# A causal depthwise convolution on the matmul engine: four token phases of 32 channels in place of two of 64, and its layer norm by tokens

## The chip, the cores and the metric

The kernel runs on one core of a Trainium2 chip. Its time is the device time of one execution in microseconds. The number to predict is the median of several runs. The engines are TensorE (PE, with its weight loads as PEld), VectorE (DVE), ScalarE (ACT), GpSimd (POOL) and SyncE (SP, which here only issues transfers).

## The reference

Two transformer-like blocks follow each other, each with two layers, on 256 tokens of width 1024, all in float32. The change touches only the mixer of the first block, twice (layers 0 and 1). One mixer projects the normed tokens, and from the projection it makes three parts: sparse attention (512 wide), a gated depthwise convolution (256 channels) and a pooled part (256 wide). The three go through `w_out`.

```python
def conformer_conv(u, conv_dw, conv_b, ln_g, ln_b, conv_pw):
    a, g = jnp.split(u, 2, axis=-1)
    y = a * jax.nn.sigmoid(g)
    y = lax.conv_general_dilated(          # 31 taps, causal, one filter for each of 256 channels
        y, conv_dw[:, None, :], window_strides=(1,), padding=[(CONV_KERNEL - 1, 0)],
        dimension_numbers=('NWC', 'WIO', 'NWC'), feature_group_count=CONV_WIDTH)
    y = y + conv_b
    y = jax.nn.silu(layernorm(y, ln_g, ln_b))          # over the 256 channels of a token
    return jnp.einsum('bsc,cd->bsd', y, conv_pw)

        mix = jnp.concatenate([y_attn, y_conv, y_pool], axis=-1)
        mix = jnp.einsum('bse,ed->bsd', mix, w_out[i])
        h = h + rmsnorm(mix, norm_mix_post[i])
```

## The kernel before

The program is written engine by engine: each engine has its own instruction list, and the lists wait for each other through counted semaphores (`nxt(name)` waits for the next count of a semaphore, `do(..., counts[name])` raises it, `settle()` waits for the engine's own latest result). No scheduler moves anything, so the order in the code is the order on the engine.

**Weights.** All large weights stream through SBUF in chunks of 1 MB (128 partitions of 2048 values), each loaded in two halves. ScalarE copies a half to a rounded high part (`prep`, tile `whi`, 128x1024), VectorE subtracts it from the original to get a low part (`lo`, tile `wlo`), and TensorE multiplies high by high, high by low and low by high, three matmuls in the place of one float32 matmul (`wide_tile`). `lo(s)` on VectorE's list therefore stands between its other work, and TensorE waits for it (`arrive`). A chunk of index `s0 + 11` is the first one of `w_out` (`s0` counts from the layer's first input chunk), `s0 + 14` its last.

**The stage of the mixer.** TensorE's list in this stage is: scores of head pairs 0 to 3 (`scores`), tap matmuls of the convolution laid between them (`taps`, as many as `TAPS_AT` says at each of five places), the turned probabilities (`turn_probs`), the products with the values (`mix_values`), and then the chunks of `w_out` (`tail`). A score goes to VectorE (`masked`: mask and row maximum), to ScalarE (`exps`) and back to VectorE (`scaled`: divide by the sum) before `turn_probs` can take it; `scores(p)` may only start when `masked(p - 1)` has read the banks.

**The convolution before.** The gated input is turned to channels by tokens, with even tokens in 64 partitions and odd tokens in the other 64 (`YT`, `YC`; 4 groups of 64 channels). One tap matmul holds a 128x128 block of taps as weights and streams 128 token pairs; 16 shifts for each of 4 groups make 64 matmuls in plain float32 a layer. The result lies channels by tokens in `acc[:, 3]`. The layer norm over channels then runs across partitions: a matmul with a matrix of 1/256 (`means`, L2058) gives the mean, VectorE subtracts it (L1264), ScalarE squares, a second matmul (L2073) gives the variance, GpSimd takes the power -0.5 (L487), VectorE spreads it (L1276), a third matmul (L2081) turns it, VectorE multiplies (L1280), ScalarE applies gain, bias and silu (L737), and 16 matmuls (`conv_out`, L2094) apply `conv_pw`. VectorE splits their result (`split`, L1172 and L1174) for the last chunk of `w_out`. Before its first half (128 tokens) of `w_out`, TensorE calls `ready(i)` for each of 8 blocks of 128 features in the order attention 0, 1, pool 0, 1, attention 2, 3, convolution 0, 1.

**Tap weights.** Each layer has 8 pieces of 8 taps (512 KB), loaded by SyncE into a ring of 4 (`load_taps`); while SyncE waits to issue a piece, the weight chunks behind it in its list wait too.

**Layer 0 alone** has one more step: after the split of the convolution VectorE computes rotary angles (`angles_by_feature`), and ScalarE's sines of these stand ahead of the squares of the norm that follows `w_out`.

## Time and profile before

| | us |
|---|---|
| median of 3 runs | 2320.17 (2319.89 to 2320.49) |
| time of the profiled execution | 2319.79 |
| its span (first to last instruction) | 2318.0 |
| TensorE busy in it | 2296.8 (99%) |
| VectorE busy in it | 1540.9 (66%) |
| ScalarE busy in it | 1221.5 (53%) |
| mean share of the DMA engines in use by the weights' queue | 56.4% |

The span is one profiled execution; what lies around it is the 1.8 us between 2318.0 and 2319.79. A time that is saved or lost on TensorE's list shows one to one in the span, since TensorE is hardly ever idle.

### The profile page before, as it was taken

What the parts mean: (1) busy time and instruction counts of PE and PEld (TensorE: products, weight loads), DVE (VectorE), ACT (ScalarE), POOL (GpSimd) and SP (SyncE); (2) the same over time, 40 slices, a digit from 0 to 9 for tenths busy, and PEclk for the clock granted to TensorE, in tenths of its full rate; (3) what the DMA queues carried; (4) which work ended last, traced back from release to release, by engine and by line L of the source; (5) the groups of instructions that cost most, each with busy time, mean ns of one, the idle gap of its engine ahead of it and who ended that gap; (6) DMA issues with size and microseconds to landing.
All of it is one profiled execution on the core that took longest, in us unless ns stands there. A gap on an engine that the chain in (4) does not pass through costs nothing.

```text
span 2318.0 us, 30390 instructions
## 1 busy us (share of the span) xinstructions
PE 2296.8 (99%) x12124; PEld 1959.9 (85%) x12124; DVE 1540.9 (66%) x2019; ACT 1221.5 (53%) x1788; POOL 79.1 (3%) x134
## 2 busy tenths in 40 slices
PE   8999999999999999999999999999999999999998
PEld 6888888888888888988888888888889888888887
DVE  6867657776566667876575665665678765756664
ACT  6645446464455556755444554554567553445553
POOL 0110000100000000000000000000000000000000
PEclk9999999999999999999999999999999999999999
DMA  8437655456656555645665465565556456554652
GB/s 334 146 119 238 198 171 209 146 170 203 211 163 217 189 172 163 206 162 183 218 199 191 157 217 192 179 221 190 173 164 214 153 183 221 195 193 164 199 193 89
DMA packets 119805, 434.91 MB, mean 188 GB/s; under 512 B 13553, under 2 KB 13809, under 8 KB 119665
## 3 DMA queue, kind: packets, MB, share of 16 engines
q1 hardware_dynamic: 119664, 432.96, 56.4%
q8 instruction: 97, 1.59, 0.3%
q14 instruction: 44, 0.35, 0.0%
HBM read 431.86 MB, written 1.05 MB: 187 GB/s over the span
## 4 chain that ended last, share of the span: by engine, by line
PE 95%; DVE 4%; ACT 1%; issue 0%; POOL 0%; DMA 0%; DVEq 0%; POOLq 0%; ACTq 0%
PE ub L1716 21%; PE ub L1713 11%; PE ub L1684 9%; PE ub L1686 9%; PE ub L1685 9%; PE acc L1684 8%; PE acc L1685 8%; PE acc L1686 8%; PE ub L1691 1%; PE ub L1692 1%; PE ub L1693 1%; PE acc L1747 1%; DVE wlo L1020 1%; DVE work L1208 1%; PE acc L2162 0%; DVE best L1205 0%
## 5 line engine op out<-in xcount | busy, mean ns | idle before, releaser
L1020 DVE TENSOR_TENSOR wlo<-raw,whi 128x1024 fp32r<-128x1024 f32 x776 | 913.1, 1220 | 215.2 <-ACT whi L534 213.4
L534 ACT ACTIVATE whi<-raw 128x1024 fp32r<-128x1024 f32 x776 | 777.3, 1052 | 200.9 <-PE ub L1686 140.5
L1716 PE MATMUL ub<-xhl,whi 128*128 128x512 f32 x2176 | 514.6, 390 | 0.0
L1716 PEld LDWEIGHTS ub<-xhl,whi 128*128 128x128 f32 x2176 | 404.2, 188 | 82.7 <-issue 1.3
L1684 PE MATMUL acc<-whi,bhl 128*128 128x512 f32 x736 | 288.2, 392 | 0.0
L1685 PE MATMUL acc<-wlo,bhl 128*128 128x512 f32 x736 | 286.6, 389 | 0.0
L1686 PE MATMUL acc<-whi,bhl 128*128 128x512 f32 x736 | 286.5, 389 | 0.0
L1684 PE MATMUL ub<-whi,xhl 128*128 128x512 f32 (+1 forms) x704 | 275.3, 391 | 3.0 <-DVE wlo L1020 1.5
L1713 PEld LDWEIGHTS ub<-xhl,wlo 128*128 128x128 f32 x2176 | 272.0, 191 | 6.2
L1713 PE MATMUL ub<-xhl,wlo 128*128 128x256 f32 x2176 | 275.4, 283 | 0.0
L1686 PE MATMUL ub<-whi,xhl 128*128 128x512 f32 (+1 forms) x704 | 272.5, 387 | 0.0
L1685 PE MATMUL ub<-wlo,xhl 128*128 128x512 f32 (+1 forms) x704 | 272.4, 387 | 0.0
L1686 PEld LDWEIGHTS acc<-whi,bhl 128*128 128x128 f32 x736 | 138.2, 188 | 29.0
L1684 PEld LDWEIGHTS acc<-whi,bhl 128*128 128x128 f32 x736 | 138.3, 188 | 27.9
L1685 PEld LDWEIGHTS acc<-wlo,bhl 128*128 128x128 f32 x736 | 138.3, 188 | 27.4
L1684 PEld LDWEIGHTS ub<-whi,xhl 128*128 128x128 f32 x704 | 132.7, 189 | 30.7 <-issue 1.8
L1686 PEld LDWEIGHTS ub<-whi,xhl 128*128 128x128 f32 x704 | 132.6, 188 | 26.6
L1685 PEld LDWEIGHTS ub<-wlo,xhl 128*128 128x128 f32 x704 | 132.8, 189 | 25.2
L1427 DVE TENSOR_TENSOR tX<-tS,ub 128x512 f32<-128x512 f32 x72 | 49.5, 687 | 132.6 <-ACT tS L839 132.4
L839 ACT ACTIVATE tS<-ub 128x512 f32<-128x512 f32 x72 | 43.0, 597 | 149.2 <-PE ub L1713 124.6
L1684 PE MATMUL ub<-whi,bhl 128*128 128x512 f32 x256 | 99.8, 390 | 0.0
L1686 PE MATMUL ub<-whi,bhl 128*128 128x512 f32 x256 | 99.6, 389 | 0.0
(305 smaller groups left out, 2471.7 us busy)
## 6 DMA issues: line engine op xcount, KB each, us to landing
raw<-in_w SPq DMA_DIRECT2D x776, 512.0 KB, 5.0
gain<-in_gains SPq DMA_DIRECT2D x20, 512.0 KB, 7.8
tapw<-in_taps SPq DMA_DIRECT2D x16, 512.0 KB, 4.3
DEC<-in_decay SPq DMA_DIRECT2D x2, 768.0 KB, 8.1
par<-in_par SPq DMA_DIRECT2D x2, 647.0 KB, 9.4
par<-in_par SPq DMA_DIRECT2D x2, 556.0 KB, 7.2
H<-in_x SPq DMA_DIRECT2D x2, 512.0 KB, 4.5
out_h<-H SPq DMA_DIRECT2D x4, 256.0 KB, 2.6
```

The costliest lines, as they stand in the source:

```text
L534: do(act.activation(whi[:, s % RING, c], raw[:, slot, c], ACT.Copy), counts["w_hi"])
L839: do(act.activation(units(tS[:, j % 2, :]), ub[:, 2 * (j % 2):2 * (j % 2) + 2, 0:S], ACT.Copy), counts["a_out"])
L1020: do(dve.tensor_tensor(wlo[:, s % RING, c], raw[:, PLACES[s][0], c], whi[:, s % RING, c].bitcast(f32), ALU.subtract), counts["w_lo"])
L1208: do(dve.match_replace(after[:, c0:c1], best[:, t, :], cur[:, c0:c1], TAKEN))
L1427: do(dve.tensor_tensor(units(tX[:, j % 2, :]), units(tS[:, j % 2, :]), ub[:, 2 * (j % 2):2 * (j % 2) + 2, S:2 * S], ALU.add), counts["us"])
L1684: pe.matmul(o, x_h, w_h, start=first, stop=False, skip_group_check=True)
L1685: pe.matmul(o, x_h, w_l, start=False, stop=False, skip_group_check=True)
L1686: return pe.matmul(o, x_l, w_h, start=False, stop=last, skip_group_check=True)
L1691: pe.matmul(o, w_h, x[:, 0, :], start=first, stop=False, skip_group_check=True)
L1692: pe.matmul(o, w_h, x[:, 1, :], start=False, stop=False, skip_group_check=True)
L1713: last = pe.matmul(bank[:, S:], wlo[:, s % RING, n:n + P], xhl[:, kt, 0, :], start=first, stop=stop, skip_group_check=True)
L1716: last = pe.matmul(bank, whi[:, s % RING, n:n + P], xhl[:, kt, :, :].rearrange("p a n -> p (a n)"), start=first, stop=stop, skip_group_che ...
```

## The change

Tokens now lie in four phases (token number modulo 4) of 32 partitions each, so 128 partitions hold 32 channels, and 8 groups of channels with 9 shifts make 72 tap matmuls a layer. The operands change places: the shifted input (64 quads of tokens, 64 columns) is the weight, and the 128x128 block of taps streams. The result lies by tokens: 64 partitions (quads), and in the free dimension 4 phases of 256 channels, gathered from two banks. The layer norm then runs along the free dimension: VectorE adds the bias as it reads the banks (`biased`), sums (L1262) and negates the mean (L1264), ScalarE squares with an accumulated sum (4 instructions), GpSimd takes the power, VectorE applies mean and deviation (4 instructions, L1280), TensorE turns the result to channels by tokens (`turn_normed`, 8 transposes), ScalarE applies gain, bias and silu, and `conv_out` is 4 matmuls of 256 columns. Both are called inside the first half of `w_out`: `turn_normed` ahead of block 4, `conv_out` ahead of block 5 (before: `last_values` after block 1, `conv_out` ahead of block 4). `TAPS_AT` puts 40 of the taps between the first and the second scores. VectorE's `lo` of the chunks `s0 + 12` to `s0 + 14` moves later in its list, and ScalarE's `prep(s0 + 14)` too. There are 9 tap pieces, and the ring has 5.

```diff
-GROUPS = 4
-SHIFTS = 16
+GROUPS = 8
+SHIFTS = 9
...
-TAP_RING = 4
-PAIRS = S // 2
+TAP_RING = 5
+QUADS = S // 4
 RSPAN = 384
-TAPS_AT = (16, 16, 12, 12, 8)
+TAPS_AT = (40, 16, 8, 8, 0)
...
                             sp.wait_ge(sem["dots_done"], IDX_HEADS * (L + 1))
-                            load_taps(L, 2, PIECES)
+                            load_taps(L, 2, 4)
+                            sp.wait_ge(sem["ze"], 7 * L + 7)
+                            load_taps(L, 4, PIECES)
...
-                    def even_and_odd(b):
+                    def phases():
 
                         nxt("yt_done")
-                        for i in range(2):
-                            r = slice(64 * i, 64 * i + 64)
-                            src = acc[r, b, :].rearrange("p (g m i) -> p g m i", g=2, i=2)[:, :, :, i]
-                            do(act.activation(YC[r, 2 * b:2 * b + 2, SHIFTS - 1:], src, ACT.Copy),
-                               counts["yc_ready"] if i else None)
+                        for g in range(4):
+                            src = acc[32 * g:32 * g + 32, 0, :].rearrange("p (f m i) -> p f m i", f=2, i=4)
+                            for i in range(4):
+                                do(act.activation(YC[32 * i:32 * i + 32, 2 * g:2 * g + 2, SHIFTS - 1:], src[:, :, :, i], ACT.Copy),
+                                   counts["yc_ready"] if i == 3 else None)
...
-                        if p == 1:
-                            prep(s0 + 14)
...
-                    nxt("ha_ready")
-                    do(act.activation(tS[:, 0, :], wide(cacc, 0, GROUPS), ACT.Square), counts["sq_ready"])
+                    nxt("cneg_ready")
+                    for j in range(4):
+                        do(act.activation(tS[0:QUADS, j // 2, (j % 2) * S:(j % 2 + 1) * S], cacc[0:QUADS, j, :], ACT.Square,
+                                          bias=cneg[0:QUADS, j:j + 1], accum_out=csq[0:QUADS, j:j + 1]),
+                           counts["sq_ready"] if j == 3 else None)
+                    attended(1)
                     act.wait_ge(sem["spare_ready"], 1)
                     do(act.activation(spare[:, 1:2], spare[:, 0:1], ACT.Silu))
...
+                    prep(s0 + 14)
+                    nxt("ct_done")
+                    for f in range(2):
+                        do(act.activation(cact[:, f, :], ub[:, 2, f * S:(f + 1) * S], ACT.Silu,
...
...
+                    def biased():
+
+                        dve.wait_ge(sem["par_in"], 16 * (L + 1))
+                        dve.wait_ge(sem["pool_out"], L + 1)
+                        dve.wait_ge(sem["tap_used"], PIECES * (L + 1))
+                        for b, bank in enumerate((3, 1)):
+                            row = par1[0:QUADS, P1["conv_b"] + b * P:P1["conv_b"] + (b + 1) * P]
+                            do(dve.tensor_tensor(
+                                cacc[0:QUADS, :, cols(b)].rearrange("p j (g c) -> p g j c", c=32),
+                                acc[0:QUADS, bank, :].rearrange("p (g j c) -> p g j c", g=4, c=32),
+                                row.rearrange("p (g c) -> p g c", c=32).unsqueeze(2).broadcast_to([QUADS, 4, 4, 32]),
+                                ALU.add), counts["c_ready"])
+
                     masked(0)
                     masked(1)
                     scaled(0)
-                    lo(s0 + 12)
+                    lo(s0 + 12, 0)
                     masked(2)
                     scaled(1)
-                    lo(s0 + 13, 0)
                     masked(3)
                     scaled(2)
-                    lo(s0 + 13)
+                    lo(s0 + 12)
+                    biased()
                     scaled(3)
-                    lo(s0 + 14, 0)
...
+                    do(dve.tensor_reduce(csum[0:QUADS, :], cacc[0:QUADS, :, :], AX.X, ALU.add))
+                    settle()
+                    do(dve.tensor_scalar(cneg[0:QUADS, :], csum[0:QUADS, :], -1.0 / S, None, ALU.mult), counts["cneg_ready"])
                     attended_lo(0)
+                    lo(s0 + 13, 0)
                     nxt("aux_ready")
...
+                    attended_lo(1)
+                    lo(s0 + 13)
+                    nxt("rstd_ready")
+                    settle()
+                    for j in range(4):
+                        do(dve.tensor_scalar(cacc[0:QUADS, j, :], cacc[0:QUADS, j, :], cneg[0:QUADS, j:j + 1],
+                                             crs[0:QUADS, j:j + 1], ALU.add, ALU.mult),
+                           counts["cn_ready"] if j == 3 else None)
                     lo(s0 + 14)
-                    nxt("rstd_ready")
...
...
-                            last = pe.matmul(acc[:, 3, cols(g)], tapw[piece % TAP_RING][:, k, :], YC[:, g, q:q + PAIRS],
-                                             start=q == 0, stop=q == SHIFTS - 1)
+                            last = pe.matmul(acc[0:QUADS, (3, 1)[g % 2], cols(g // 2)], YC[:, g, q:q + QUADS],
+                                             tapw[piece % TAP_RING][:, k, :], start=q == 0, stop=q == SHIFTS - 1)
...
+                    def turn_normed():
+
+                        nxt("cn_ready")
+                        fill(U_[2], "sig_ready")
+                        for f in range(2):
+                            for j in range(4):
+                                c = f * S + j * QUADS
+                                last = pe.transpose(ub[:, 2, c:c + QUADS], cacc[0:QUADS, j, cols(f)],
+                                                    ident[0:QUADS, 0:QUADS])
+                        give(last, "ct_done")
...
                     def made(i):
                         if i == 4:
+                            turn_normed()
+                        if i == 5:
                             conv_out()
                         pe.wait_ge(sem["prod_ready"], 4 * L + i // 2 + 1)
                     tail(so, lambda i: OUT_ORDER[i], acc_bank, lambda: turn(0, acc_bank, XN1, "xn_ready"),
-                         ready=made, first=last_values, early=1)
+                         ready=made)
```

Smaller edits: the turned input has 4 transposes in place of 8, the gated product on VectorE is written once instead of twice (256 columns instead of 512), GpSimd no longer fills `means`, and the parameter block is smaller (`P1` ends at 1030 in place of 1294).

The first place is TensorE's list in layer 0, from the first scores to the first turned probabilities (`L1900` and `L1901` are the scores, `L2003` the turned probabilities, `L2036` the taps). Before:

```order
L1901 MATMUL ub<-KK,Q 128x256
L2036 MATMUL acc<-YC,tapw_95 128x128 x8
L2036 MATMUL acc<-YC,tapw_96 128x128 x8
L1900 MATMUL ub<-KK,Q 128x128
L1901 MATMUL ub<-KK,Q 128x256
L1900 MATMUL ub<-KK,Q 128x128
L1901 MATMUL ub<-KK,Q 128x256
L2036 MATMUL acc<-YC,tapw_97 128x128 x8
L2036 MATMUL acc<-YC,tapw_98 128x128 x8
L2003 MATMUL ub<-cst,sm 128x128 x6
```

Now (the scores are L1901 and L1902, the turned probabilities L2002):

```order
L2036 MATMUL acc<-tapw_92,YC 64x128 x8
L2036 MATMUL acc<-tapw_93,YC 64x128 x8
L2036 MATMUL acc<-tapw_94,YC 64x128 x8
L2036 MATMUL acc<-tapw_95,YC 64x128 x8
L2036 MATMUL acc<-tapw_96,YC 64x128 x8
L1901 MATMUL ub<-KK,Q 128x128
L1902 MATMUL ub<-KK,Q 128x256
L1901 MATMUL ub<-KK,Q 128x128
L1902 MATMUL ub<-KK,Q 128x256
L2036 MATMUL acc<-tapw_92,YC 64x128 x8
L2036 MATMUL acc<-tapw_93,YC 64x128 x8
L2002 MATMUL ub<-cst,sm 128x128 x6
```

The second scores stand behind 40 taps instead of 16; of the 72 taps only 16 are left for the places behind the second turned probabilities and the third scores.

The second place is VectorE's list in layer 0 behind the third `scaled` (`L1237` and `L1240` are `scaled`, `L1020` is `lo`, `L1264` the mean's subtraction, `L1246` the low part of an attention block, `L1269`, `L1172` and `L1174` the pooled part). Before:

```order
L1020 TENSOR_TENSOR wlo<-raw,whi 128x1024
L1237 RECIPROCAL rinv<-rsum 128x4
L1240 TENSOR_TENSOR sm<-sm,rinv 128x2x128
L1240 TENSOR_TENSOR sm<-sm,rinv 128x2x256
L1020 TENSOR_TENSOR wlo<-raw,whi 128x1024
L1264 TENSOR_TENSOR cacc<-cacc,acc 128x512
L1246 TENSOR_TENSOR bhl<-acc,bhl 128x512
L1269 TENSOR_SCALAR tX<-ub,par_75 128x256 x2
L1172 CAST bhl<-tX 128x512
L1174 TENSOR_TENSOR bhl<-tX,bhl 128x512
```

Now (`L1225` and `L1228` are `scaled`, `L1010` is `lo`, `L1244` is `biased`):

```order
L1010 TENSOR_TENSOR wlo<-raw,whi 128x1024
L1244 TENSOR_TENSOR cacc<-acc,par_74 64x4x4x32 x2
L1225 RECIPROCAL rinv<-rsum 128x4
L1228 TENSOR_TENSOR sm<-sm,rinv 128x2x128
L1228 TENSOR_TENSOR sm<-sm,rinv 128x2x256
L1262 TENSOR_REDUCE cstat<-cacc 64x4
L1264 TENSOR_SCALAR cstat<-cstat 64x4
L1234 TENSOR_TENSOR bhl<-acc,bhl 128x512
L1010 TENSOR_TENSOR wlo<-raw,whi 128x1024
L1269 TENSOR_SCALAR tX<-ub,par_74 128x256 x2
L1160 CAST bhl<-tX 128x512
L1162 TENSOR_TENSOR bhl<-tX,bhl 128x512
```

The bias additions now stand ahead of the last `scaled`, and the sum over channels between it and the attention block.

The third place is TensorE's list in the first half of `w_out`, around the end of the convolution. Before, with `conv_out` as L2094:

```order
L1684 MATMUL acc<-whi,bhl 128x512
L1685 MATMUL acc<-wlo,bhl 128x512
L1686 MATMUL acc<-whi,bhl 128x512
L2094 MATMUL ub<-cact,par_75 128x128 x16
L1684 MATMUL acc<-whi,bhl 128x512
```

Now, with the 8 transposes as L2071 and `conv_out` as L2082:

```order
L2071 MATMUL ub<-cst,cacc 128x64 x8
L1685 MATMUL acc<-whi,bhl 128x512
L1686 MATMUL acc<-wlo,bhl 128x512
L1687 MATMUL acc<-whi,bhl 128x512
L1685 MATMUL acc<-whi,bhl 128x512
L1686 MATMUL acc<-wlo,bhl 128x512
L1687 MATMUL acc<-whi,bhl 128x512
L2082 MATMUL ub<-cact,par_74 128x256 x4
L1685 MATMUL acc<-whi,bhl 128x512
```

Between the 8 transposes and `conv_out` stands one block of `w_out` (6 matmuls); ahead of the last two blocks only one block is left behind `conv_out`, where there were two.

## Rows read from the trace of the kernel before

**Rows 1.** The page, part 1: busy us (share of the span) xinstructions, whole execution.

```profile
PE 2296.8 (99%) x12124; PEld 1959.9 (85%) x12124; DVE 1540.9 (66%) x2019; ACT 1221.5 (53%) x1788; POOL 79.1 (3%) x134
```

**Rows 2.** Two stretches (layers 0, 1): length, busy us by engine, clock, DMA share, GB/s.

```profile
85.33:128.70 43.37, 41.58 (x320) 34.78 (x320) 33.36 (x66) 20.77 (x54) 9.47 (x10) 1.00 0.50 171
421.50:464.90 43.40, 41.67 (x321) 34.80 (x320) 30.43 (x57) 20.92 (x55) 9.47 (x10) 1.00 0.49 170
```

**Rows 3.** Timeline of TensorE, layer 0: start, us, line, shapes, xcount, [idle before <-releaser].

```profile
86.19 3.84 PE L2036 MATMUL acc<-YC,tapw 128*128 128x128 f32 x32
...
101.13 0.87 PE L2003 MATMUL ub<-cst,sm 128*128 128x128 f32 x6 [0.94 <-DVE sm L1240]
101.94 0.50 PE L1900 MATMUL ub<-KK,Q 64*128 64x128 f32 x4
...
102.80 0.87 PE L2017 MATMUL acc<-turned_w,V 128*64 128x256 f32 x8
103.60 2.94 PE L2036 MATMUL acc<-YC,tapw 128*128 128x128 f32 x24
106.38 0.82 PE L2003 MATMUL ub<-cst,sm 128*128 128x128 f32 x6
```

**Rows 4.** Timeline of TensorE in two very narrow windows, inside the first value products.

```profile
103.07 0.39 PE L2017 MATMUL acc<-turned_w,V 128*64 128x256 f32 x2
...
103.28 0.39 PE L2017 MATMUL acc<-turned_w,V 128*64 128x128 f32 x4
```

**Rows 5.** Timeline of TensorE, layer 0: the norm's matmuls and `conv_out`.

```profile
111.43 1.06 PE L2058 MATMUL acc<-cacc,means 128*128 128x128 f32 x8
...
114.08 1.05 PE L2073 MATMUL acc<-means,tS 128*128 128x2 f32 x8
...
117.92 0.49 PE L2081 MATMUL acc<-cst,spread 128*128 128x128 f32 x2
...
121.09 2.06 PE L2094 MATMUL ub<-cact,par 64*128 64x128 f32 x32
```

**Rows 6.** Timeline of VectorE, layer 0: mask, scale, `lo`, attention block, pooled part.

```profile
102.93 0.96 DVE L1225 SCALAR_TENSOR_TENSOR sm<-ub,bias 128x768 f32<-128x768 f32 x1 [0.71 <-PE ub L1901]
...
105.05 1.03 DVE L1240 TENSOR_TENSOR sm<-sm,rinv 128x256 f32<-128x256 f32 x2
105.99 1.22 DVE L1020 TENSOR_TENSOR wlo<-raw,whi 128x1024 fp32r<-128x1024 f32 x1
...
113.18 0.68 DVE L1246 TENSOR_TENSOR bhl<-acc,bhl 128x512 fp32r<-128x512 f32 x1
113.78 0.87 DVE L1269 TENSOR_SCALAR tX<-ub,par 128x256 f32<-128x256 f32 x2
...
115.75 0.15 DVE L1273 TENSOR_SCALAR cvar<-acc 128x2 f32<-128x2 f32 x1
```

**Rows 7.** Groups by line and form, 80 to 140 us: xcount | busy us, mean ns.

```profile
L699 ACT ACTIVATE sm<-sm,rmax 128x256 f32<-128x256 f32 x8 | 3.9, 494 | 0.0
L1230 DVE TENSOR_REDUCE rmax<-sm 128x2 f32<-128x512 f32 x4 | 2.7, 676 | 0.0
L487 POOL TENSOR_TENSOR crs<-cvar,half 128x2 f32<-128x2 f32 x1 | 1.6, 1621 | 21.3 <-DVE cvar L1273 21.3
L1108 DVE TENSOR_SCALAR ang<-posf,cst 128x256 f32<-128x256 f32 x1 | 0.4, 353 | 0.0
```

**Rows 8.** The page, part 6: tap transfers, xcount, KB each, us to landing.

```profile
tapw<-in_taps SPq DMA_DIRECT2D x16, 512.0 KB, 4.3
```

**Rows 9.** Timeline of VectorE, layer 0: the convolution's split, the next norm's product.

```profile
123.92 0.69 DVE L1174 TENSOR_TENSOR bhl<-ub,bhl 128x512 fp32r<-128x512 f32 x1
...
135.22 1.41 DVE L1061 SCALAR_TENSOR_TENSOR XN<-H,rh,gain 128x512 f32<-128x512 f32 x2 [2.05 <-POOL rh L443]
```

**Rows 10.** Timeline of TensorE, layer 0: last `w_out` chunk, then the transposes of XN.

```profile
125.94 0.39 PE L1684 MATMUL acc<-whi,bhl 128*128 128x512 f32 x1
...
136.82 0.38 PE L1747 MATMUL acc<-cst,XN 128*128 128x128 f32 x2
```

154 lines of the change are left out of this document (50 added, 104 removed).

## The prediction

> **What bounds the kernel now.** I read the page's busy shares first: TensorE is busy for 2296.8 us, 99% of the span, VectorE for 66% [rows 1]. So a change counts by what it adds to TensorE's own work, and by how much longer it makes TensorE wait. Then I read the busy time of the stage that the change touches, from the first scores to the end of the first half of `w_out` [rows 2]. It lasts 43.37 us in layer 0 and 43.40 in layer 1, TensorE is busy in 41.58 and 41.67 of it, so idle for 1.79 and 1.73; the clock is granted in full (1.00). The layers behave alike; I work out layer 0 and double it. Last I read TensorE's and VectorE's timelines in the stage: TensorE's idle time stands ahead of scores and turned probabilities, as the 0.94 ahead of 101.13 that VectorE's `scaled` ended [rows 3], and VectorE waits for TensorE's scores in turn, 0.71 ahead of 102.93 [rows 6]. The tap matmuls are what TensorE does meanwhile.
>
> **TensorE's own work, per layer.** Records here: a float32 matmul leaves two, a transpose one.
>
> Taps. 32 records take 3.84, 24 take 2.94 [rows 3]: 0.90/8, so 0.1125 each, and 64 taps cost 128 x 0.1125 = 14.4. With 64 columns as weights and 128 streamed columns the value products are the nearest rows: 256 streamed columns at 103.07 are followed by 128-column ones at 103.28, 0.21 later [rows 4]; four records of 128 columns end within 0.39, two side by side, and with a record's own length of about 0.27 (0.38 for the 256-column one, less 0.11) the pairs stand 0.11 to 0.12 apart. The time follows the streamed columns, and they stay 128. I take 0.11: 72 x 2 x 0.11 = 15.8, which is 1.4 more. Bounds: the present spacing gives 16.2 (+1.8); the rival below has half.
>
> The other rule about this operation speaks for the change. The Trainium skill, "TensorE: Matmul & The Clock Gate", section "LDWEIGHTS (loading the stationary operand)", says that a weight load's time goes with its columns, about columns/1.2 ns. By it the 64-column load is 53 ns against 107 (an estimate from that page), and if the load set the pace the taps would take 7.7 us a layer instead of 15.8. The trace bears half of it out, as the next sentences show.
>
> Variance matmuls stream only 2 columns and still stand (1.05 - 0.25)/7 = 0.114 apart [rows 5], the pace of the taps. So for 128 columns of weights the load alone costs as much as the stream, and halving it leaves the stream as the bound.
>
> Gone: 4 of 8 transposes, at (0.82 - 0.27)/5 = 0.11 each [rows 3], 0.44; the mean's 8 records 0.9 (1.06 less the tail), the variance's 0.92, the turn of the deviation 0.3 [rows 5]. Added: 8 transposes, no dearer than 0.11 each, with two changes of matmul type about 1.1 (bounds 0.6 and 1.3). `conv_out` goes from 32 records in 2.06 less the tail [rows 5] to 8 with 256 columns at 0.215, 1.8: 0.2 less. Sum: 1.4 + 1.1 - 0.44 - 0.9 - 0.92 - 0.3 - 0.2 = **-0.3**. TensorE's own work stays where it was.
>
> **TensorE's waits, per layer.** `TAPS_AT` puts 40 taps ahead of the second scores: 8.8 us, which covers `masked(0)` fully, so the present wait there goes. But VectorE has nothing to do meanwhile, and what it does later is then in a row with TensorE. Prices from VectorE's rows: from the start of `masked` at 102.93 to the end of `scaled` at 105.05 + 1.03 is 3.15 [rows 6], 3.25 with the hand-overs. On TensorE scores take 102.80 - 101.94 = 0.86, value products 0.80, turned probabilities 0.75 [rows 3], 8 taps 1.76; a change between kinds of matmul costs 0.1 (the pairs at 103.28 and 103.39 would be followed at 103.50, the taps start at 103.60 [rows 3, 4]), two of them around a run of taps 0.2.
>
> - Second turned probabilities: VectorE needs 3.25 behind the third scores, TensorE has 8 taps, 1.95. Wait **1.3**.
> - Third: behind the fourth scores again 3.25, TensorE has value products and 8 taps, 2.75. Wait **0.5**.
> - Fourth: behind `scaled(2)` VectorE has half a `lo`, 1.14 (1.22 less the overlap [rows 6]), `biased`, not in the trace, nearest the 128x512 subtraction from a bank, 0.60 from 113.18 to 113.78 [rows 6], twice 1.2 (bounds 1.1 and 2.0), and `scaled(3)` 1.15: 3.5. TensorE has 0.75 + 0.80 + 0.80, and 0.1 for a copy: 2.45. Wait **1.0** (and the 0.1).
> - The transposes of the normed result: behind `scaled(3)` VectorE works without a gap: sum over 4 x 256, from the 512-element maximum of 0.676 [rows 7] at one more ns an element 1.2 (bounds 1.0 and 1.6), mean 0.2, low part 0.6, half a `lo` 1.14, pooled part 115.75 - 113.78 = 1.97 [rows 6], variance 0.1, low part 0.6, half a `lo` 1.14, then 4 `tensor_scalar` of 256: nearest 0.353 [rows 7], overlapped 0.28, 1.1 (bounds 0.8 and 1.9). Together 8.05. TensorE has 0.75, pooled product 1.0, 0.80 and 24 matmuls of `w_out` at 10.88/48 = 0.227 (125.94 to 136.82 holds 48 [rows 10]) with 0.1: 8.1. A tie, but GpSimd's power lies beside the last low parts: 1.62 for 2 columns [rows 7], now 4, so 1.6 to 3.2; I take 1.9. Wait **0.2**.
> - Last block: VectorE's split of `conv_out`, 1.4, against one block of `w_out`, 1.4. Wait **0.1**.
>
> Sum 3.2, before 1.8: **+1.4**. With the work, **+1.1 to +1.2** a layer, 2.3 for both.
>
> **Layer 0 alone.** The split ended at 124.61, and TensorE needed it at 125.94 [rows 9, 10]: 1.3 of slack. From the split's end, angles, sines, squares and GpSimd's root led to XN at 136.63, 12.0 later [rows 9]; TensorE asked for it 10.9 after 125.94 [rows 10]. Now TensorE takes up the last block as the split ends, so the lead of 1.3 is gone: the first half of XN is ready 11.35 after, the second 12.0, against 10.9 and 11.8. Wait 0.5 + 0.2 = **0.7** (bounds 0 and 1.3). Layer 1 has no angles there, and nothing waits.
>
> **What costs nothing.** ScalarE's 16 small copies in place of 4: bounded above by the 0.494 of a 256-column one [rows 7], 4 take 2.0, and TensorE has half of the pool projection (24 matmuls, 0.11 each at least) and 0.86 of scores before the first tap; the other groups are needed 4 us apart. Without that cover the first tap would be up to 2.0 late. VectorE's two `lo` of the last chunk, 2.3, now come behind the four scalings, and TensorE has the 8 transposes, `conv_out` and two blocks, 5.8, before it needs them; without that cover they would be on the path. ScalarE's `prep` for them is done before. The tap pieces: SyncE is held until 32 taps are done, as now, but those now come in one run, so the weights behind them come no later; a piece lands in 4.3 [rows 8], and behind the issue of the last one stand 32 more taps, 7.0, before its own. Less on VectorE in the gated product (0.5) is covered, since the second scores wait for the taps.
>
> **Sum.** The profiled execution took 2319.8 (its span of 2318.0 and 1.8 around it). 2319.8 + 2.3 + 0.7 = 2322.8; the median of the runs, 2320.2, lies 0.4 above that execution. I say **2323.2**.
>
> **Rivals.**
> - *Load-bound taps (faster).* The load of 128 columns takes as long as the taps' spacing [rows 5]; if it is what sets the pace, 64 columns stand 0.055 apart. The 40 taps ahead of the second scores then take 4.4 less, the next 16 gain 0.4 until `scaled(0)` holds them, and at the later places longer waits eat the rest. 1.15 - 4.8 is 3.6 less than before a layer: 2319.8 - 7.2 + 0.7, with the 0.4, 2313.7. The sign turns below about 0.09 a record, 0.2% is passed below about 0.065. The 0.21 for 256 columns [rows 4] speaks against it. 0.06. [...]
> - *VectorE's norm chain is dearer (slower, clearly).* Sum, four scalings and power at their upper bounds add 0.4 + 0.8 + 1.0, `biased` 0.5: each lies on the chain without a gap, so up to 2.5 a layer, 2327 to 2328. For it: three of these prices stand in no row. Against: all of their nearest rows are cheap. 0.22.
> - *The waits don't add up (no change).* VectorE's steps overlap more, or the old waits were as long for the same reasons: 2319.5 to 2321. 0.17.
> - *My sum:* 2321 to 2325. 0.55.
>
> The range 2319.5 to 2327.5 leaves out the fast rival and the end of the slow one; the forecast's own is 2321 to 2325. A measurement of this kernel can tell about 0.2%, 4.6 us, from no change. Slower by more (above 2324.8): most of the slow rival and a tail of mine, 0.26. Faster by more (below 2315.5): 0.05. Within: 0.69.
>
> **What would show it.** Right: tap records about 0.11 apart with 64-column weights; TensorE's idle time in the stage near 3.2, with the longest waits ahead of the second and fourth turned probabilities, all ended by VectorE's `scaled`; VectorE idle for some us ahead of the second `masked`; in layer 0 alone a wait of 0.5 or more at the transposes of XN. Wrong: a spacing near 0.06; a wait above 1 ahead of the 8 new transposes, or one at `conv_out` ended by ScalarE; a first tap that waits for ScalarE's copies.

## The result, and the profile after

The changed kernel takes 2324.16 us (median of 20 runs, 2323.46 to 2325.78); the kernel before, run beside it, 2320.29 (20 runs, 2319.46 to 2321.29). The ratio is 1.0017, with a 95% interval of 1.0011 to 1.0023: 3.9 us slower. The interval lies above 1, so the loss is clear, though it is smaller than the 0.2% that the forecast calls a change that can be told. The profiled execution took 2324.03, its span is 2321.8. The page, part 1, of the changed kernel, in the columns of [rows 1]:

```profile
PE 2295.9 (99%) x12080; PEld 1957.7 (84%) x12080; DVE 1545.4 (67%) x2029; ACT 1226.3 (53%) x1814; POOL 77.9 (3%) x131
```

TensorE works 0.9 us less than in [rows 1] and the span is 3.8 longer: the loss is waiting. Where it lies is read from the stage in layer 0, from the first scores to the start of the last block of `w_out`. First the kernel before, then the changed one (length, PE busy, PEld, DVE, ACT, POOL, clock, DMA share, GB/s):

```profile
85.33:125.94 40.61, 38.82 (x308) 32.49 (x308) 31.12 (x61) 20.45 (x53) 9.47 (x10) 1.00 0.53 182
```

```profile
84.79:127.31 42.52, 38.38 (x290) 31.62 (x289) 32.44 (x62) 21.78 (x61) 8.84 (x10) 1.00 0.51 174
```

TensorE idles 42.52 - 38.38 = 4.14 us where it idled 40.61 - 38.82 = 1.79, and works 0.44 less. Its timeline in the changed kernel names the places (start, us, line, shapes, xcount, [idle before <-releaser]; L1901 are scores, L2002 turned probabilities, L2036 taps, L2071 the transposes of the normed result, L2082 `conv_out`, L1685 blocks of weight chunks, L1748 the transposes of XN). The lines answer to [rows 3, 5, 10]:

```profile
85.65 8.95 PE L2036 MATMUL acc<-tapw,YC 128*64 128x128 f32 x80
94.53 0.50 PE L1901 MATMUL ub<-KK,Q 64*128 64x128 f32 x4
...
99.03 0.87 PE L2002 MATMUL ub<-cst,sm 128*128 128x128 f32 x6
...
104.03 0.88 PE L2002 MATMUL ub<-cst,sm 128*128 128x128 f32 x6 [1.37 <-DVE sm L1228]
...
109.03 0.87 PE L2002 MATMUL ub<-cst,sm 128*128 128x128 f32 x6 [0.72 <-DVE sm L1228]
...
112.50 0.87 PE L2002 MATMUL ub<-cst,sm 128*128 128x128 f32 x6 [0.83 <-DVE sm L1228]
...
120.97 0.68 PE L2071 MATMUL ub<-cst,cacc 64*128 64x64 f32 x8
121.58 0.50 PE L1685 MATMUL acc<-whi,bhl 128*128 128x512 f32 x1
...
123.07 1.89 PE L2082 MATMUL ub<-cact,par 128*128 128x256 f32 x8
124.61 0.58 PE L1685 MATMUL acc<-whi,bhl 128*128 128x512 f32 x1
...
127.31 0.47 PE L1685 MATMUL acc<-whi,bhl 128*128 128x512 f32 x1 [0.95 <-DVE bhl L1162]
...
138.84 1.32 PE L1748 MATMUL acc<-cst,XN 128*128 128x128 f32 x8 [0.39 <-DVE XN L1051]
...
149.12 0.47 PE L1685 MATMUL ub<-whi,xhl 128*128 128x512 f32 x1 [0.76 <-DVE wlo L1010]
```

The 80 tap records stand (8.95 - 0.27)/79 = 0.110 us apart (0.27 is the last one's own length). Two waits of the kernel before, not among its rows above, are needed beside them:

```profile
90.61 0.50 PE L1900 MATMUL ub<-KK,Q 64*128 64x128 f32 x4 [0.58 <-DVE sm L1225]
...
146.30 0.47 PE L1684 MATMUL ub<-whi,xhl 128*128 128x512 f32 x1 [0.26 <-DVE wlo L1020]
```

The wait of 0.58 ahead of the second scores is gone; those ahead of the second to fourth turned probabilities have come for it, and one of 0.95 ahead of the last block. VectorE in the same stretch of the changed kernel:

```profile
95.52 0.96 DVE L1213 SCALAR_TENSOR_TENSOR sm<-ub,bias 128x768 f32<-128x768 f32 x1 [4.51 <-PE ub L1902]
...
110.03 1.27 DVE L1244 TENSOR_TENSOR cacc<-acc,par 64x512 f32<-64x512 f32 x2
...
112.48 1.21 DVE L1262 TENSOR_REDUCE cstat<-cacc 64x4 f32<-64x1024 f32 x1
...
119.49 1.37 DVE L1280 TENSOR_SCALAR cacc<-cacc,cstat 64x256 f32<-64x256 f32 x4
...
125.00 1.07 DVE L1160 CAST bhl<-ub 128x512 fp32r<-128x512 f32 x1 [1.86 <-PE ub L2082]
126.10 1.05 DVE L1162 TENSOR_TENSOR bhl<-ub,bhl 128x512 fp32r<-128x512 f32 x1
```

VectorE idles 4.51 ahead of the second `masked`, while TensorE does its 40 taps; that TensorE waits later for what VectorE could not do then is the theory which the first experiments test. The two instructions of the split, the second of them 0.69 in [rows 9], take 1.07 and 1.05. GpSimd's power for 4 columns (at 117.74) took 1.02, less than the 1.62 for 2 columns in [rows 7].

The sum, by how far TensorE's list lags behind that of the kernel before: the first scores come 0.54 earlier, the last block 1.37 later, the transposes of XN 2.02 later [rows 10], and the block at 149.12 (146.30 before) 2.82 later. In layer 1 the same stage adds 1.96 (the last block at 466.54 against 462.12, the first scores at 424.02 against 421.56), and XN's transposes stand at 477.51 against 473.00. From there the 4.5 stay to the last matmul. From its start to the end of the span it is 6.1 us where it was 6.7, which leaves the 3.8 (3.9 before rounding). These 0.6 us less come back in the trace of every run with the new convolution, against every one with the old; what shortens the end of the program was not looked into. So TensorE's list does not show one to one in the span here: 0.6 of its loss is given back behind it.

### The profile page after: what moved, and what is told of

It reads as the page before. It is cut to its first block, busy times and chain, and to the rows that moved or that the text cites. A ratio compares the mean times of both kernels' runs of the same rounds, so it can differ in the third digit from the quotient of the medians.

```text
span 2321.8 us, 30325 instructions
## 1 busy us (share of the span) xinstructions
PE 2295.9 (99%) x12080; PEld 1957.7 (84%) x12080; DVE 1545.4 (67%) x2029; ACT 1226.3 (53%) x1814; POOL 77.9 (3%) x131
## 3 DMA queue, kind: packets, MB, share of 16 engines
HBM read 432.64 MB, written 1.05 MB: 187 GB/s over the span
## 4 chain that ended last, share of the span: by engine, by line
PE 96%; DVE 2%; ACT 0%; issue 0%; DMA 0%; POOL 0%; SPq 0%; DVEq 0%; POOLq 0%; ACTq 0%
PE ub L1717 21%; PE ub L1714 11%; PE ub L1685 9%; PE ub L1687 9%; PE ub L1686 9%; PE acc L1685 9%; PE acc L1687 8%; PE acc L1686 8%; PE ub L1692 1%; PE ub L1693 1%; PE ub L1694 1%; PE acc L2036 1%; PE acc L1748 1%; DVE wlo L1010 1%; PE ub L1902 0%; PE acc L2152 0%
## 5 line engine op out<-in xcount | busy, mean ns | idle before, releaser
L1010 DVE TENSOR_TENSOR wlo<-raw,whi 128x1024 fp32r<-128x1024 f32 x776 | 913.7, 1221 | 215.0 <-ACT whi L529 213.5
L1685 PE MATMUL acc<-whi,bhl 128*128 128x512 f32 x736 | 288.7, 392 | 1.9 <-DVE bhl L1162 1.9
L1685 PE MATMUL ub<-whi,xhl 128*128 128x512 f32 (+1 forms) x704 | 275.3, 391 | 3.7 <-DVE wlo L1010 1.9
L1685 PEld LDWEIGHTS acc<-whi,bhl 128*128 128x128 f32 x736 | 138.3, 188 | 30.7 <-issue 3.1
L1685 PEld LDWEIGHTS ub<-whi,xhl 128*128 128x128 f32 x704 | 132.7, 188 | 31.6 <-issue 2.3
L1685 PE MATMUL ub<-whi,bhl 128*128 128x512 f32 x256 | 99.8, 390 | 0.0
```

The costliest lines, as they stand in the source:

```text
L1010: do(dve.tensor_tensor(wlo[:, s % RING, c], raw[:, PLACES[s][0], c], whi[:, s % RING, c].bitcast(f32), ALU.subtract), counts["w_lo"])
L1685: pe.matmul(o, x_h, w_h, start=first, stop=False, skip_group_check=True)
```

## The experiments

My theory, from the two traces: three separate things make the new waits. The order of the taps (`TAPS_AT`) gives TensorE 40 taps where fewer would cover VectorE's step, and 8 where VectorE needs about 16; the split writes with a step (its elements do not lie side by side); and in layer 0 the rotary angles, which VectorE computes behind the split, hold what follows. The rivals: the waits are VectorE's work as a whole, which would show elsewhere if one were removed; or the convolution and its norm themselves are dearer. Each time stands beside the kernel before as run on the same chip in the same rounds, whose median was 2320.2 in the first four runs, 2321.4 in the next four, and 2320.3 and 2320.1 in the last. The 95% intervals of these ratios reach about 2 us to either side, so smaller differences between two runs are not shown by the times alone; for them I go by the traces.

**The taps, in both kernels.** The changed kernel with another order:

```diff
-TAPS_AT = (40, 16, 8, 8, 0)
+TAPS_AT = (24, 16, 16, 16, 0)
```

> The changed kernel with TAPS_AT = (24, 16, 16, 16, 0) in place of (40, 16, 8, 8, 0). Mine (the order of the taps, not the convolution itself, costs the waits ahead of the turned probabilities): 24 taps, 5.3 us, still cover the first masked step, VectorE's idle time of 4.51 ahead of the second one falls to about 1.0, and 16 taps, 3.65 with the hand-over, cover the 3.25 that VectorE needs behind the third and fourth scores: the waits of 1.37 and 0.72 go to 0 and 0.1. The fourth, 0.83, goes to 0 to 0.4. 2.3 to 2.9 us a layer, 2318.3 to 2319.6 in all, under the kernel before. Rival (the waits are VectorE's whole work per layer, which no order of the taps shortens, so they come back at the transposes of the normed result): the stage stays as long, waits of 1 to 2 us ahead of the 8 transposes or of conv_out, 2322 to 2324.

2320.13 us, ratio 1.0000 (0.9991 to 1.0008): all of the loss is gone. The three waits of 1.37, 0.72 and 0.83 went, but one of 0.96 came ahead of the first turned probabilities:

```profile
96.79 0.88 PE L2002 MATMUL ub<-cst,sm 128*128 128x128 f32 x6 [0.96 <-DVE sm L1228]
```

Its cause is seen on VectorE (first fence; L1213 and L1218 are `masked`) and GpSimd (second):

```profile
92.25 0.96 DVE L1213 SCALAR_TENSOR_TENSOR sm<-ub,bias 128x768 f32<-128x768 f32 x1 [1.01 <-PE ub L1902]
93.24 1.01 DVE L1218 TENSOR_REDUCE rmax<-sm 128x2 f32<-128x256 f32 x2
...
94.37 2.36 DVE L1228 TENSOR_TENSOR sm<-sm,rinv 128x256 f32<-128x256 f32 x2
96.66 1.21 DVE L1010 TENSOR_TENSOR wlo<-raw,whi 128x1024 fp32r<-128x1024 f32 x1
```

```profile
91.65 3.12 POOL L477 TENSOR_TENSOR PO<-W,cst 64x256 f32<-64x256 f32 x4
94.85 1.33 POOL L480 TENSOR_TENSOR PO<-PO,UP 128x512 f32<-128x512 f32 x1
```

`scaled(0)` now falls beside GpSimd's pooling and takes 2.36, where the later `scaled` take 1.03. So the gain was 3.9 and not 4.6 to 5.8.

The kernel before with the changed kernel's order:

```diff
-TAPS_AT = (16, 16, 12, 12, 8)
+TAPS_AT = (36, 12, 8, 8, 0)
```

> The kernel before with only TAPS_AT = (36, 12, 8, 8, 0) in place of (16, 16, 12, 12, 8), the changed kernel's order for its 64 taps. Mine: the wait of 0.58 ahead of the second scores goes, but 8 taps, 1.8 us, stand where 12 stood ahead of the third and fourth turned probabilities, and VectorE has half a low part more there than in the changed kernel: waits of 1.8 to 2.5 ahead of the third and 1 to 1.5 ahead of the fourth, 1.3 to 2.0 a layer in all, 2323 to 2324.5. Rival (the place of the taps is indifferent, since VectorE's work as a whole decides): 2320 to 2321, with the idle time of TensorE in the stage at 1.8 as before.

2322.94, ratio 1.0013 (1.0004 to 1.0022): 2.8 us slower, with the old convolution. TensorE's waits:

```profile
98.95 0.88 PE L2003 MATMUL ub<-cst,sm 128*128 128x128 f32 x6 [0.39 <-DVE sm L1240]
...
104.51 0.87 PE L2003 MATMUL ub<-cst,sm 128*128 128x128 f32 x6 [1.83 <-DVE sm L1240]
...
109.51 0.88 PE L2003 MATMUL ub<-cst,sm 128*128 128x128 f32 x6 [0.48 <-DVE sm L1240]
```

The pattern follows the order of the taps, whichever convolution they belong to. The two larger waits stand one place earlier than I had written, ahead of the second and third turned probabilities, and the second of them is smaller than my 1 to 1.5.

**The split.** In the changed kernel:

```diff
-split(*(z[:, 4:6, :].rearrange("p f (m j) -> p f j m", j=4) for z in (bhi, blo)),
-      ub[:, 0, :].rearrange("p (f j m) -> p f j m", f=2, j=4), "prod_ready")
+split(*(z[:, 4:6, :].rearrange("p f (m j) -> p f m j", j=4) for z in (bhi, blo)),
+      ub[:, 0, :].rearrange("p (f j m) -> p f m j", f=2, j=4), "prod_ready")
```

> The changed kernel, with only the two instructions that split conv_out taken in the order of the result (channel block, token, phase) in place of (channel block, phase, token), so that they write without a step, as the kernel before did. Mine (the step of four elements on the written side makes each 1.07 and 1.05 us where the kernel before has 0.69): both fall to about 0.69, the split ends 0.7 to 0.75 us earlier, and TensorE's wait ahead of the last block of w_out falls from 0.95 to 0.2 in both layers; XN of layer 0 comes 0.7 earlier too, so its wait stays. 1.4 to 1.6 us faster than the changed kernel, about 2322.6. Rival (the price is that of reading one bank in place of two, or of the pattern of three dimensions, whatever the order): the two stay at 1.05 and the time at 2324. Rival (the wait belongs to what VectorE does ahead, two low parts of a weight chunk): the wait stays near 0.9 although the two get shorter.

2322.62, ratio 1.0011 (1.0002 to 1.0020), 2.5 above the kernel before where the changed one is 3.9 above. What got shorter is in the trace, VectorE's first and then TensorE's:

```profile
125.48 0.69 DVE L1160 CAST bhl<-ub 128x512 fp32r<-128x512 f32 x1 [1.86 <-PE ub L2082]
126.20 0.69 DVE L1162 TENSOR_TENSOR bhl<-ub,bhl 128x512 fp32r<-128x512 f32 x1
```

```profile
127.04 0.47 PE L1685 MATMUL acc<-whi,bhl 128*128 128x512 f32 x1 [0.21 <-DVE bhl L1162]
```

As expected to a tenth: both fell to 0.69, and the wait of 0.95 to 0.21. The other way round in the kernel before, which has two phases and so a step of two elements:

```diff
-split(*(z[:, 4:6, :].rearrange("p f (m j) -> p f m j", j=2) for z in (bhi, blo)),
-      ub[:, 0:2, 0:S].rearrange("p j (f m) -> p f m j", f=2), "prod_ready")
+split(*(z[:, 4:6, :].rearrange("p f (m j) -> p f j m", j=2) for z in (bhi, blo)),
+      ub[:, 0:2, 0:S].rearrange("p j (f m) -> p f j m", f=2), "prod_ready")
```

> The kernel before with its split of conv_out taken by channel block, phase and token, so that it writes with a step of two elements (8 bytes) and reads each bank in a row, the other way round than it does. The changed kernel writes with a step of four (16 bytes) and takes 1.07 and 1.05 in place of 0.69. Theory A (each element that is written into another group of 16 bytes pays): with two elements in a group they stay at 0.69. Theory B (any step on the written side pays): above 0.8. In either case TensorE has 1.3 of slack ahead of the last block, and the time stays at 2320 to 2321.

A single run, 2319.97, and both instructions stay at 0.69:

```profile
123.41 0.69 DVE L1172 CAST bhl<-ub 128x512 fp32r<-128x512 f32 x1 [3.46 <-PE ub L2094]
124.14 0.69 DVE L1174 TENSOR_TENSOR bhl<-ub,bhl 128x512 fp32r<-128x512 f32 x1
```

So for this split a step of 8 bytes on the written side is free, and one of 16 costs half as much again (1.07 and 1.05 against 0.69): theory A. The order of reading is not the cause: the changed kernel and this run both read their banks in a row, one at 1.07 and the other at 0.69. The Trainium skill, "SBUF — State Buffer", section "Door 1: The DMA port swizzle (why `[64,N]` ≈ `[32,N]`)", says that SBUF has lines of 16 bytes, that two accesses in a row to a line are needed for full speed, and that each crossing to a new line pays. These three measurements agree; where the same place counts steps of up to 4 float32 as free, they do not, since the step of 4 is the one that paid.

**The angles of layer 0.** First into VectorE's idle time (the cut leaves out the lines that give their tiles other places, three in `tX`):

```diff
...
                     masked(0)
+                    if L == 0:
+                        angles_by_feature()
                     masked(1)
...
-                    if L == 0:
-                        angles_by_feature()
                     for t in range(2):
```

> The changed kernel with the angles of layer 0 (3.8 us of VectorE) computed ahead of the second masked step, where VectorE idles 4.51, in place of behind the split of conv_out; three of their tiles lie in tX for that, two in the place of the old result of the convolution. Mine (the angles and the sines behind them are what makes layer 0 dearer than layer 1): no new wait at the second masked step, ScalarE squares as soon as the first 12 matmuls of the last block are done, 1.7 earlier, the waits of 0.4 and 0.25 ahead of the two halves of XN's transposes go, and of the 0.76 ahead of w_lo at 149 at least 0.5. 1.0 to 1.4 us faster than the changed kernel, 2322.8 to 2323.2. Rival (the chain of squares, root and XN behind the last block decides by itself): 0 to 0.3.

2324.76, ratio 1.0021 (1.0012 to 1.0029): 4.6 above the kernel before, where the changed one is 3.9 above. These 0.7 lie inside the interval, and the trace does not show them: from the first scores of layer 0 to the transposes of XN in layer 1 TensorE's list takes 392.6 us, and 392.7 in the changed kernel. So nothing was gained. On VectorE two instructions of the same form and size:

```profile
92.63 0.76 DVE L1069 TENSOR_SCALAR tX<-tX 128x256 f32<-128x256 f32 x1
...
97.80 0.29 DVE L1080 TENSOR_SCALAR ycos<-tX 128x256 f32<-128x256 f32 x1
```

The first stands beside GpSimd's pooling, the second behind its end at 96.2. The angles took 6.9 in place of 3.8 and put a wait of 2.0 ahead of the first turned probabilities:

```profile
101.41 0.88 PE L2002 MATMUL ub<-cst,sm 128*128 128x128 f32 x6 [2.00 <-DVE sm L1228]
```

The waits at XN and at `w_lo` did go, so this run does not tell what the angles are worth. The next one puts them where GpSimd stands still: among the last `w_down` chunks of the feed-forward stage (number 12, and ScalarE's sines at 13). The cut shows VectorE's part; the tiles lie in the place of `trig2`:

```diff
...
                             lo(min(s + 3, sf + 31))
+                            if L == 0 and j == 12:
+                                angles_by_feature()
```

> The changed kernel with only the angles of layer 0 and their sines moved to the last w_down chunks of the first feed-forward stage. Where the angles stood in the run before, beside GpSimd's pooling, they took 6.85 us in place of 3.75, which hid the gain behind a new wait of 2.0; here GpSimd stands still. Mine (in layer 0 the angles hold the squares of the last block, XN and the low parts behind them): the waits of 0.39 and 0.25 ahead of the transposes of XN and of 0.76 ahead of w_lo go, 1.3 to 2.1 us faster than the changed kernel, 2322.0 to 2322.9; the angles take 3.75 again. Rival (the chain of squares and root holds XN alone): 0 to 0.3.

2323.34, ratio 1.0009 (1.0001 to 1.0018), 1.9 above the kernel before. TensorE's waits from 120 to 160 us (total, times, longest):

```profile
PE acc L1685 <- DVE bhl L1162: 1.0, 1, 1.0
PE ub L2071 <- issue: 0.2, 1, 0.2
```

The changed kernel has 0.4 at XN and 0.8 at `w_lo` there too. So the angles were worth 2.0 us, in layer 0 alone; the table further down has 2.07 from the traces. (The median itself, 2323.34, lies above the 2322.0 to 2322.9 that I expected: in these rounds the kernel before took 1.2 longer too.)

**The taps themselves.** Two of the four output phases are left out here:

```diff
-last = pe.matmul(acc[0:QUADS, (3, 1)[g % 2], cols(g // 2)], YC[:, g, q:q + QUADS],
-                 tapw[piece % TAP_RING][:, k, :], start=q == 0, stop=q == SHIFTS - 1)
+c = (g // 2) * P
+last = pe.matmul(acc[0:QUADS, (3, 1)[g % 2], c:c + 64], YC[:, g, q:q + QUADS],
+                 tapw[piece % TAP_RING][:, k, 0:64], start=q == 0, stop=q == SHIFTS - 1)
```

> The changed kernel with 64 of the 128 columns streamed in each tap matmul, so that two of the four output phases of the convolution are left out; the 64 columns of weights stay. Mine (the streamed columns set the pace, the load of the weights ran beside them at half their time): a record goes from 0.110 to 0.055 to 0.06, 40 taps end 4.3 to 4.4 earlier, VectorE's steps then set the stage, with 1 us more of wait ahead of the first turned probabilities: about 3.4 a layer, 2317 to 2318. Rival (a record costs 0.11 whatever its columns, as the 2-column variance matmuls with 128 columns of weights did): the spacing stays 0.11, the time 2324.

A single run, 2321.94. The spacing was as I said, the time was not. TensorE's timeline:

```profile
85.86 4.88 PE L2037 MATMUL acc<-tapw,YC 128*64 128x64 f32 x80
...
100.95 1.54 PE L2002 MATMUL ub<-cst,sm 128*128 128x128 f32 x6 [2.69 <-DVE sm L1228]
102.43 0.81 PE L1901 MATMUL ub<-KK,Q 64*128 64x128 f32 x4
```

(4.88 - 0.22)/79 = 0.059 a record with both sides at 64 columns, 0.110 with 64 of weights and 128 streamed, 0.1125 with 128 on both [rows 3]. So with 64 columns of weights it is not their load that sets the pace of the taps but the streamed columns. The first turned probabilities came 3.6 earlier (95.45 against 99.03), as expected; then the second waited 2.69, and what stood behind that wait ran slower (the last section comes back to it), so that 1.7 were left at the last block.

**The edits together,** the first step towards a better version:

> The changed kernel with three edits together: the split of conv_out in the order of its result (minus 1.5 by itself), TAPS_AT = (24, 16, 16, 16, 0) (minus 4.0 by itself), and the angles of layer 0 moved from behind the split to the last w_down chunks of the first feed-forward stage, in the place of trig2, where they are needed only at the end of the layers. If the three waits are separate: 2324.2 - 1.5 - 4.0 - 1.4 to 2.1 = 2316.6 to 2317.3, faster than the kernel before by 0.12 to 0.16%. Rival (each is only handed on to the next wait): no better than the best single edit, 2320. TensorE's idle time from the scores to the last block of w_out 1.1 to 1.5 a layer, all of it the wait ahead of the first turned probabilities (0.96) and the last block (0.2).

2317.99, ratio 0.9987 (0.9978 to 0.9996), 3.4 under the kernel before, which was 1.2 slower in these rounds than in those I had worked from. Against the changed kernel, 3.9 above the kernel before, the three edits gain 3.9 - 2.5 = 1.4 (split), 3.9 (taps) and 3.9 - 1.9 = 2.0 (angles), 7.3 in all, and together 3.9 + 3.4 = 7.3. With intervals of 2 us to either side, that the times agree to a tenth is luck. The traces say the same without them, by when TensorE starts the first scores of layer 0 and the transposes of XN in layer 1:

| | scores, layer 0 | XN, layer 1 | between | gain |
|---|---|---|---|---|
| changed kernel | 84.79 | 477.51 | 392.72 | |
| split by token | 85.28 | 476.49 | 391.21 | 1.51 |
| taps later | 85.01 | 473.68 | 388.67 | 4.05 |
| angles late | 84.80 | 475.45 | 390.65 | 2.07 |
| all three | 84.56 | 469.71 | 385.15 | 7.57 |

The single gains add up to 7.63, and together they give 7.57: they are separate waits, not one that moves.

**The old convolution with a better order,** first the taps, then the angles as well (the same edit as above):

```diff
-TAPS_AT = (16, 16, 12, 12, 8)
+TAPS_AT = (20, 16, 16, 12, 0)
```

> The kernel before with only TAPS_AT = (20, 16, 16, 12, 0) in place of (16, 16, 12, 12, 8): the last 8 taps move ahead, to the places where TensorE waits. Mine: 4 more taps, 0.9, cover the 0.58 ahead of the second scores, 4 more cover the 0.94 ahead of the second turned probabilities, and the place without taps stays covered by value products: 1.2 to 1.5 a layer, 2317.2 to 2318, so a better order of the taps gives the old convolution as much as the new one, and the convolution itself is worth nothing. Rival (the later start of the second scores is handed on, as VectorE's steps beside GpSimd are slow): 0.5 a layer or less, 2319 to 2320.

> The old convolution with the same surroundings, for a comparison of the two at their best: TAPS_AT = (20, 16, 16, 12, 0), which by itself was 3.0 under the kernel before, and the angles moved to the last w_down chunks. Only a wait of 0.25 ahead of w_lo was left in that run in layer 0, so 0 to 0.4 is to be gained: 3.0 to 3.4 under the kernel before. If so, and the run with GpSimd's pooling later comes out at 5.0 to 5.4 under it, the new convolution is worth 1.6 to 2.4 us once the waits around it are gone, and the forecast's term for TensorE's own work (minus 0.3 a layer) was too small; if both come out alike, the term was right or too large.

The taps alone: 2318.45, 3.0 under the kernel before (ratio 0.9987, 0.9978 to 0.9996), as much as the 1.2 to 1.5 a layer that I expected. With the angles: 2316.56, 3.8 under it (0.9985, 0.9976 to 0.9994) where I had expected 3.0 to 3.4, and the list of TensorE's waits from 84 to 152 us is empty.

**GpSimd's pooling.** To the run with three edits one wait is added on GpSimd, ahead of its four multiplications:

```diff
                     settle()
+                    pool.wait_ge(sem["scaled"], 4 * L + 1)
                     for f in range(2):
```

> The three edits of the run with split, taps and angles together, and one more: GpSimd's four multiplications of the pooled sums wait until VectorE has scaled the first two heads' probabilities. In that run scaled(0), two instructions with both operands in SBUF, took 2.36 us beside GpSimd in place of 1.03, and TensorE waited 0.96 ahead of the first turned probabilities. If GpSimd is the cause: scaled(0) takes 1.03, the wait of 0.96 falls below 0.1 in both layers, the half of w_lo behind it takes longer (up to 2.3 in place of 1.22), which the 0.7 us of idle time ahead of masked(2) and the 16 taps mostly cover: 1.5 to 1.9 us faster than that run, 5.0 to 5.4 under the kernel before. Rival (the delay is only moved to w_lo, masked(2) and the second turned probabilities): a wait of 0.5 to 1.0 there, 0 to 0.5 faster. Rival (scaled(0) is slow for another reason, such as the first use of the tile): 2.36 stays.

2315.97, ratio 0.9983 (0.9974 to 0.9992): 4.4 under the kernel before, 0.9 better than without, not 1.5 to 1.9 (by the two points of the table 0.6: 85.93 to 470.51). VectorE, GpSimd and TensorE:

```profile
95.29 1.03 DVE L1229 TENSOR_TENSOR sm<-sm,rinv 128x256 f32<-128x256 f32 x2
...
100.60 2.09 DVE L1229 TENSOR_TENSOR sm<-sm,rinv 128x256 f32<-128x256 f32 x2
```

```profile
96.47 3.98 POOL L478 TENSOR_TENSOR PO<-W,cst 64x256 f32<-64x256 f32 x4 [3.97 <-DVE sm L1229]
100.52 1.28 POOL L481 TENSOR_TENSOR PO<-PO,UP 128x512 f32<-128x512 f32 x1
```

```profile
102.74 0.87 PE L2003 MATMUL ub<-cst,sm 128*128 128x128 f32 x6 [0.68 <-DVE sm L1229]
```

`scaled(0)`, the pair at 95.29, is back at 1.03, so GpSimd was the cause. But its last instruction now meets `scaled(1)`, and a wait of 0.68 came back ahead of the second turned probabilities, where my rival had it, though not through `w_lo`. The last run lets the first two multiplications go at once:

```diff
-                    pool.wait_ge(sem["scaled"], 4 * L + 1)
                     for f in range(2):
+                        if f:
+                            pool.wait_ge(sem["scaled"], 4 * L + 1)
```

> As the run with GpSimd's pooling later, but only the second two of its four multiplications wait until scaled(0) is done; the first two go at once, while VectorE waits or reads scores from PSUM. There GpSimd ended at 101.8, 1.2 after scaled(1) began at 100.60, and scaled(1) took 2.09 in place of 1.03, with a wait of 0.68 ahead of the second turned probabilities. With two multiplications (1.6 to 2.0 us) out of that stretch GpSimd ends near 100. If the meeting of the two engines is all that is left of that wait: scaled(0) and scaled(1) both take 1.03, no wait above 0.25 is left in the stage, 1.0 to 1.4 us faster than that run, 5.3 to 5.8 under the kernel before. Rival (the later start of GpSimd is handed on to w_lo and masked(2)): 0 to 0.4 faster, with w_lo above 2 us.

2314.56, ratio 0.9976 (0.9966 to 0.9985), 5.6 under the kernel before, as expected, and the fastest of all. `scaled(0)` and `scaled(1)` are both short now (first fence), and of TensorE's waits two small ones are left in each layer (second fence, layer 1, 420 to 480 us):

```profile
94.03 1.03 DVE L1230 TENSOR_TENSOR sm<-sm,rinv 128x256 f32<-128x256 f32 x2
...
99.33 1.03 DVE L1230 TENSOR_TENSOR sm<-sm,rinv 128x256 f32<-128x256 f32 x2
```

```profile
PE acc L1687 <- DVE bhl L1164: 0.2, 1, 0.2
PE ub L2073 <- issue: 0.2, 1, 0.2
```

## Why the prediction held, and where its terms were off

Forecast 2323.2 (2319.5 to 2327.5), measured 2324.2; "my sum" (2321 to 2325) was the case that came. The mechanism was the one I gave, and the order of the taps is shown to be its main part: undone alone it gives back 3.9 us. That the number came so close is in part luck, since terms that were off by more offset each other. Term by term, a layer:

- *Waits, plus 1.4.* Measured 4.14 - 1.79 = 2.35 more. Second, third and fourth turned probabilities 1.3, 0.5, 1.0: 1.37, 0.72, 0.83. Transposes of the normed result 0.2: 0.13, too short to be listed (the matmul before ends at 120.84, they start at 120.97). Up to there the sum is right, 3.0 against 2.9.
- *Last block 0.1: 0.95.* This is the term that was furthest off. I took the split at its old 1.4 without looking at how the new one writes; it takes 2.1, and the slack of 1.3 that it had before is gone. Of it 0.74 a layer is the written step, as the run with the split by token shows (0.95 to 0.21).
- *TensorE's own work, minus 0.3.* Measured 0.44 in the stage and 0.43 ahead of it (in layer 1 the lag falls from 420.62 - 417.73 = 2.89 at the turned input to 424.02 - 421.56 = 2.46 at the scores), minus 0.9. The page has 0.9 less for both layers together, since TensorE's busy time in the other stretches is 0.8 longer. The taps are as predicted. The 8 transposes take 0.61 (121.58 - 120.97) and not 1.1, `conv_out` 1.54 (124.61 - 123.07) and not 1.8. This hid most of the error above. With almost no waits left in either kernel, the time is 5.6 under the kernel before with the new convolution and 3.8 with the old. These 1.8 lie inside the intervals, and the end of the program has 0.6 of them. In the traces TensorE's list between the two points of the table is 1.0 shorter with the new one (84.67 to 467.69 against 85.43 to 469.40), and 0.4 of layer 0 lie ahead of the first point: 1.4, or 0.7 a layer, with two waits of 0.2 a layer still in it.
- *Layer 0, plus 0.7.* Measured 2.82 - 1.37 = 1.45. The part at XN was 0.93 with its second half (behind the transposes the lag is 139.91 - 137.61 = 2.30). The rest is the wait for `w_lo` at 149.12, 0.5 longer than before (0.76 against 0.26); I had not followed the angles that far.
- *The end of the program,* not in the sum: 0.6 shorter, once. Without it the loss would have been about 4.5.
- *What costs nothing* did cost nothing: the first taps wait for no copy of ScalarE and no piece, and the two `lo` behind the scalings are done before TensorE asks.

Of the rivals, load-bound taps are excluded by 0.110 and by the run with half the columns. The dearer norm chain did not come: sum 1.21 and biases 1.20 from start to start as I had them, the four scalings 1.3 (1.1), the power 1.02 (1.9). That the waits do not add up is excluded by the three edits, which do. Of the signs of being right, two came only in part: the idle time in the stage was 4.14 and not near 3.2, with the wait at the last block, ended by the split, its second longest; and at XN the first wait was 0.39, the 0.5 being passed only with the second half.

## What to carry to other kernels

When filler work on the bound engine is laid between the steps of a chain with another engine, its worth depends on where it lies: price the chain's answer at each place and give each place that much, since what is left over at one place cannot be used at the next. When a layout changes, check on which side the copies that follow it now step, and by how many bytes. A stretch in which VectorE idles is not free for other work while GpSimd works in it, as `scaled` and the angles showed.

## What the runs showed that I had not expected

**VectorE beside GpSimd.** The pair of instructions of `scaled`, both operands in SBUF, took 2.36 and 2.09 us beside GpSimd's `tensor_tensor`, and 1.03 otherwise; a `tensor_scalar` of 256 columns within SBUF took 0.76 against 0.29. `masked`, which reads scores from PSUM, kept its 0.96, and the maximum its 1.01, in the same stretch (92.25 and 93.24 in the run with the taps later). The other way round GpSimd's four multiplications went from 3.12 to 3.98 behind a `w_lo` of VectorE that had begun a little earlier (96.24 against 96.47) and kept its 1.22. The Trainium skill, "SBUF — State Buffer", section "Who interferes with whom", says that the two engines share a pair of ports under an exclusive lock, that VectorE instructions with two inputs in SBUF, and those in its two-port modes, contend for it with GpSimd, and that the order of issue decides who is held up. The traces agree for `scaled`, `masked` and the multiplications behind `w_lo`; in which mode the `tensor_scalar` ran they do not show.

**The clock.** In the run with half the streamed columns TensorE did 0.31 us of work from 98 to 101 us (it waited 2.69), and its granted clock then fell from 1.00 to 0.50, which is 1.2 in place of 2.4 GHz; its longest gap in the stage until then had been 1.09. Length and columns are as in the two stretches of the result:

```profile
98.00:101.00 3.00, 0.31 (x6) 0.17 (x4) 2.83 (x6) 1.21 (x6) 0.00 (x0) 0.85 1.03 418
101.00:103.00 2.00, 2.00 (x10) 1.67 (x12) 0.00 (x0) 1.11 (x5) 0.00 (x0) 0.50 0.17 70
...
107.30:110.00 2.70, 2.54 (x22) 1.61 (x22) 2.67 (x5) 2.16 (x6) 0.00 (x0) 1.00 0.11 27
```

Six turned probabilities took 1.54 there in place of 0.87. The second turned probabilities came 3.1 earlier than in the changed kernel (100.95 against 104.03), the third only 1.7 (107.35 against 109.03). Other waits left the clock at 1.00: those of 1.37 in the changed kernel, and the one of 2.00 ahead of 101.41 in the run with the angles early, whose granted clock from 101 to 103 us was 1.00. Why it fell in the one run and not in the others was not looked into.
